# RWKV chunk inverse without GpSimd, and modulation blocks spread over all units, in a two-layer hybrid diffusion step

## What is computed

```python
m = silu(cond) @ w_mod + b_mod            # per layer, split in 6 vectors of 1024
kk = k * k_k;  kk = kk * rsqrt(sum(kk * kk) + 1e-12)
for d in (forward, backward):
    decay = exp(-exp(-softplus(-(w0[d] + tanh(h @ w1[d]) @ w2[d])) - 0.5))
    a = sigmoid(a0[d] + (h @ a1[d]) @ a2[d])
    k_d = k * (1 + (a - 1) * k_a)
    # scan over tokens, per head, S is 64x64:
    S = S * decay + (S @ -kk) (kk * a)^T + v k_d^T;   y = S @ r
```

## Time and profile before

| | |
|---|---|
| median of 3 runs | 2732.68 us (2728.0 to 2733.49) |
| the profiled execution | 2720.77 us, span of its instructions 2719.0 us, granted TensorE clock 0.975 |
| RWKV phases | about 300 to 635 us (layer 0) and 1465 to 1785 us (layer 1) |
| TensorE, VectorE, ScalarE, GpSimd busy | 92%, 53%, 39%, 11% |
| chain that ended last | TensorE 81%, VectorE 11%, issue 3%, ScalarE 3% |

### The profile page before, as it was taken

One profiled execution on the slowest core, in us unless ns is written; L12 is line 12 of the kernel. 1 busy time (PEld: TensorE's weight loads), 2 busy tenths in 40 slices (PEclk: granted clock), 3 DMA queues, 4 the chain that ended last, 5 costly groups with the idle time before them and its releaser, 6 DMA issues.

```text
span 2719.0 us, 67961 instructions
## 1 busy us (share of the span) xinstructions
PE 2492.1 (92%) x30324; PEld 2193.1 (81%) x30324; DVE 1449.9 (53%) x2522; ACT 1068.6 (39%) x1926; POOL 306.5 (11%) x307
## 2 busy tenths in 40 slices
PE   6998789988999999989987888888999999999996
PEld 3996577776798998969965767767999999999995
DVE  2337556666533333362375657665565555555565
ACT  3226433334421212242254334344444444444452
POOL 0002123330000000010011333301100000000011
PEclk8999899999999999989998999998999999999998
DMA  7223123200122222212200330002765666666572
GB/s 274 78 78 127 38 91 127 103 28 6 70 78 78 73 76 78 78 66 78 72 16 2 127 127 4 4 5 82 268 211 179 214 210 209 182 211 212 180 260 82
DMA packets 82700, 304.57 MB, mean 112 GB/s; under 512 B 9376, under 2 KB 9504, under 8 KB 82272
## 3 DMA queue, kind: packets, MB, share of 16 engines
q1 hardware_dynamic: 71072, 257.93, 28.8%
q0 software_dynamic: 11328, 42.21, 4.2%
HBM read 273.11 MB, written 27.00 MB: 110 GB/s over the span
## 4 chain that ended last, share of the span: by engine, by line
PE 81%; DVE 11%; issue 3%; ACT 3%; DMA 1%; POOL 1%; SPq 0%; DVEq 0%; ACTq 0%; POOLq 0%
PE ps L451 19%; PE ps L452 19%; PE ps L453 19%; PE ps L1181 6%; PE ps L464 2%; PE ps L915 2%; PE ps L810 1%; PE ps L958 1%; PE ps L1113 1%; PE ps L974 1%; DMA ring<-in_blocks 1%; PE ps L818 1%; DVE arena L2451 1%; DVE arena L2450 1%; PE ps L463 1%
## 5 line engine op out<-in xcount | busy, mean ns | idle before, releaser
L2258 DVE TENSOR_TENSOR ring_lo<-ring,w_ffn 128x1024 fp32r<-128x1024 f32 x264 | 322.4, 1225 | 214.4 <-ACT w_ffn L1700 208.7
L451 PE MATMUL ps<-hg_hi,w_ffn 128*128 128x256 f32 x1408 | 401.6, 285 | 0.9 <-DVE hg_lo L2891 0.9
L452 PE MATMUL ps<-hg_lo,w_ffn 128*128 128x256 f32 x1408 | 397.2, 282 | 0.0
L453 PE MATMUL ps<-hg_hi,ring_lo 128*128 128x256 f32 x1408 | 396.7, 282 | 0.0
L1700 ACT ACTIVATE w_ffn<-ring 128x1024 fp32r<-128x1024 f32 x264 | 278.2, 1057 | 197.8 <-PE ps L453 197.5
L451 PEld LDWEIGHTS ps<-hg_hi,w_ffn 128*128 128x128 f32 x1408 | 266.5, 189 | 2.6 <-DVE hg_lo L2891 1.1
L452 PEld LDWEIGHTS ps<-hg_lo,w_ffn 128*128 128x128 f32 x1408 | 265.6, 189 | 1.2
L453 PEld LDWEIGHTS ps<-hg_hi,ring_lo 128*128 128x128 f32 x1408 | 266.2, 189 | 0.0
L1181 PEld LDWEIGHTS ps<-arena 64*64 64x64 f32 x7680 | 168.8, 139 | 72.6 <-issue 63.1
L453 PE MATMUL ps<-hT_ffn_hi,ring_lo 128*128 128x320 f32 x704 | 215.5, 306 | 0.0
L451 PE MATMUL ps<-hT_hi,w_proj 128*128 128x320 f32 x672 | 205.7, 306 | 7.0 <-DVE hT_lo L2264 6.9
(11 more groups left out here) (379 smaller groups left out, 5205.0 us busy)
## 6 DMA issues: line engine op xcount, KB each, us to landing
ring<-in_blocks SPq DMA_DIRECT2D x484, 512.0 KB, 3.7
h_rows<-arena POOLq DMA_DIRECT2D x16, 512.0 KB, 10.2
arena<-h_rows POOLq DMA_DIRECT2D x7, 1024.0 KB, 11.1
y_rows<-arena POOLq DMA_DIRECT2D x7, 1024.0 KB, 6.6
x<-in_x_all SPq DMA_DIRECT2D x1, 2560.0 KB, 13.4
h_plain<-arena POOLq DMA_DIRECT2D x1, 2560.0 KB, 16.0
out_y_all<-x POOLq DMA_DIRECT2D x5, 512.0 KB, 3.6
w<-in_low POOLq DMA_DIRECT2D x2, 768.0 KB, 6.4
```

The costliest lines, as they stand in the source:

```text
L451: nc.tensor.matmul(dst, w_hi, m_hi, start=start, stop=False)
L452: nc.tensor.matmul(dst, w_hi, m_lo, start=False, stop=False)
L453: return nc.tensor.matmul(dst, w_lo, m_hi, start=False, stop=stop)
L2258: V.tensor_tensor(ring_lo[:, n % RING, :], ring[:, n % RING, :], high[:, n % high.shape[1], :], ALU.subtract).then_inc(*E.sig("w_lo"))
```

## The change

`plus_eye` is gone from GpSimd. ScalarE now copies N^T and N of both halves, and X of half 0; VectorE makes I + N^T of both halves, after ScalarE's copy, and copies X of half 1. VectorE's scan step now stands ahead of its work on the inverse in each slot. The copy to `qf` moves from VectorE to ScalarE. The scaled tanh of `prep` (L2560) moves to ScalarE, which writes it into `k_dec`; VectorE multiplies it by k in slot 5 instead of 6, and ScalarE's exponentials of slot 5, which overwrite `k_dec`, wait for that product. GpSimd keeps x0, lw and kds. In layer 0 an even unit has two groups of modulation and an odd one one; in layer 1 each unit has one. The blocks stand in slots 4 to 9, the rows in 7 and 10, the turns in 8 and 11. Each unit ends with a wait for its last modulation.

```diff
@@ slots and groups
+        def mod_groups(g):
+            if g is None:
+                return []
+            if g < UNITS:
+                at = MOD_FIRST + 3 * (g // 2) + 2 * (g % 2)
+                return [at, at + 1] if g % 2 == 0 else [at]
+            return [MOD_MID + g - UNITS]
+
+        def mod_slots(g):
+            return [((4, 4, 5, 6), 7, 8), ((6, 7, 8, 9), 10, 11)] if len(mod_groups(g)) == 2 else [((4, 6, 8, 9), 10, 11)]
@@ TensorE, rwkv_second
-                    if m0 is not None:
-                        if s == 4:
-                            if n is not None:
-                                pe.wait_ge(sem["ta_ev"], n + 1)
-                                pe.wait_ge(sem["vt_ev"], n // 2 + 1)
-                        if 4 <= s <= 7:
-                            for q in range(2):
-                                mod_block(2 * (s % 2) + q, 6 if s < 6 else 7)
-                        if s in (7, 8):
-                            mod_turn(m0 + s - 7, s - 1)
+                    if a is not None and s == 4 and n is not None:
+                        pe.wait_ge(sem["ta_ev"], n + 1)
+                        pe.wait_ge(sem["vt_ev"], n // 2 + 1)
+                    for k, (m, (blocks_at, row_at, turn_at)) in enumerate(zip(mod_groups(a), mod_slots(a))):
+                        for q in range(4):
+                            if blocks_at[q] == s:
+                                mod_block(q, 6 + k)
+                        if turn_at == s:
+                            mod_turn(m, 6 + k)
@@ ScalarE, decay_rest
-                A(kdt[:, :], pair640(src), ACT.Tanh, bias=..., scale=0.5).then_inc(*E.sig("ta_ev"))
+                A(kdt[:, :], pair640(src), ACT.Tanh, bias=..., scale=0.5).then_inc(*E.sig("act_step"))
+                act.wait_ge(*E.own_last())
+                if n >= 1:
+                    act.wait_ge(sem["tk_tr"], 3 * n)
+                A(k_dec[:, :], kdt[:, :], ACT.Identity, bias=hpar[:, 36 + c:37 + c], scale=hpar[:, 32 + c:33 + c]).then_inc(*E.sig("ta_ev"))
@@ ScalarE, exps, s == 5
                     act.wait_ge(sem["dec_cum"], 2 * n + 2)
+                    act.wait_ge(sem["kd_ev"], n + 1)
@@ ScalarE, rwkv_first, ahead of the copies of wu
+                    if d == 0:
+                        A(qf[:, 1, :], st_in[:, c, d, :], ACT.Copy).then_inc(*E.sig("qf_ev"))
+                    else:
+                        act.wait_ge(sem["dec_ph"], b + 1)
+                        A(qf[:, 1, :], st_in[:, c, d, :], ACT.Copy, scale=phs[:, b % 3, NCH:NCH + 1]).then_inc(*E.sig("qf_ev"))
@@ ScalarE, rwkv_second
-                    if a is not None and level <= 5 and half == 0:
-                        t, tx = half_tiles(0), x_tiles(0)
+                    if a is not None and level <= 5:
+                        t, tx = half_tiles(half), x_tiles(half)
                         act.wait_ge(sem["lv_mm"], LV_UNIT * a + s)
-                        A(by_head(nt_m[:, whole(t), :, :]), in_banks(0, 1, len(t)), ACT.Copy).then_inc(*E.sig("nt0_ev"))
+                        A(by_head(nt_m[:, whole(t), :, :]), in_banks(half, 1, len(t)), ACT.Copy).then_inc(*E.sig("nt_ev"))
                         if level <= 4:
+                            done = "n1_ev" if half else "lv0_ev" if level == 1 else "act_step"
+                            A(by_head(n_m[:, whole(t), :, :]), in_banks(half, 0, len(t)), ACT.Copy).then_inc(*E.sig(done))
-                        if level >= 2:
+                        if level >= 2 and half == 0:
                             A(by_head(xt[:, whole(tx), :, :]), in_banks(0, 2, len(tx)), ACT.Copy).then_inc(*E.sig("lv0_ev"))
@@ VectorE, rwkv_first: the copy to qf is gone; rwkv_second, behind the scan step
-                        V.tensor_copy(by_head(nt_m[:, whole(t), :, :]), in_banks(1, 1, len(t))).then_inc(*E.sig("nt1_ev"))
-                            V.tensor_copy(by_head(n_m[:, whole(t), :, :]), in_banks(1, 0, len(t))).then_inc(...)
+                    if a is not None and level <= 4:
+                        t = whole(half_tiles(half))
+                        dve.wait_ge(sem["nt_ev"], NT_UNIT * a + s)
+                        V.tensor_tensor(s_m[(level + 1) % 2][:, t, :, :], nt_m[:, t, :, :], eye_all[:, t, :, :], ALU.add).then_inc(*E.sig("s_ev"))
+                    if a is not None and 2 <= level <= 5 and half == 1:
+                        ...
+                        V.tensor_copy(by_head(xt[:, whole(tx), :, :]), in_banks(1, 2, len(tx))).then_inc(*E.sig("lv1_ev"))
@@ VectorE, prep
-                    V.tensor_scalar(kdt[:, :], kdt[:, :], hpar[:, 32 + c:33 + c], hpar[:, 36 + c:37 + c], ALU.mult, ALU.add).then_inc(*E.sig("dve_step"))
-                if s == 6:
-                    dve.wait_ge(*E.own_last_of("dve_step"))
-                    V.tensor_tensor(kdt[:, :], kdt[:, :], kr, ALU.mult).then_inc(*E.sig("kd_ev"))
+                    V.tensor_tensor(kdt[:, :], k_dec[:, :], kr, ALU.mult).then_inc(*E.sig("kd_ev"))
@@ GpSimd, rwkv_phase
-                        for s in range(1, 5):
-                            plus_eye(a, (s + 1) // 2, (s + 1) % 2)
-                    if a is not None:
-                        for s in range(5, 9):
-                            plus_eye(a, (s + 1) // 2, (s + 1) % 2)
```

## The result

The change makes the kernel slower: 2747.74 us (2743.95 to 2757.23) against 2728.26 (2722.34 to 2733.49), a ratio of 1.0078 with the interval 1.0063 to 1.0093. The forecast was 2725.3, its range ended at 2743. The profiled execution took 2743.95 us, span 2742.1.

The account below looks back on a forecast made before the run. The prediction took TensorE, busy 92% of the span, to bound the kernel. Its terms, -12.8 - 0.2 + 1.4 + 4.2 = -7.4 us, taken from 2732.7, gave 2725.3 us, range 2706 to 2743.

Parts of the forecast that it names:

- The second rival of the prediction: ScalarE's wait for the kd product does not bite, slot 8 stays at t = 14.9: 2709 us, chance 0.16.
- the placement: Modulation spread over the units, some blocks free in waits, 1.65 us more per one-group unit; -11.5 us in all.
- the inverse's later s8: I + N^T on VectorE, copies on ScalarE: slot 8 comes later in units without modulation before; +16 us in all.
- qf to ScalarE: Copy leaves VectorE, so L2487 follows L2474 at once: 0.85 us gained in each of 14 units.
- The walk to s8: Chain of handovers from prefix sums to slot 8: starts at t = 17.05 or 16.95 instead of 14.9, 2.1 us later.
- The price of a block: A modulation block costs TensorE 0.52 us, half of a pair's time; in slot 8, 0.38 of it is covered.
- Code: TensorE stops for its own code where short products stay dense behind slot 8: +4.2 us, between 0 and 16.
- the third rival: Code takes the gain: fewer waits turn into TensorE stops, one more of 0.9 us in 9 units; 2733 us, chance 0.14.
- Units of 38.0 and 39.0: Unit lengths in us with one and two modulation groups; units 1 to 6: -12.8 in layer 0, -0.2 in layer 1.
- First and last units: First unit of a layer unchanged; last unit's new modulation group partly fills TensorE's code stops, +0.7 us in each layer.
- The clock: TensorE's granted clock falling to its lower level: the prediction's sum had no term for it.
- The first rival: The new chain costs more: slot 8 another 1.5 us later in 14 units, 21 us; 2746 us, chance 0.22.

Follow-up runs that it names:

- e3: The kernel before with only the copy to qf moved from VectorE to ScalarE; ratio to before 0.9975.
- e10: The kernel before with the qf copy on ScalarE and the modulation spread as in the change, old inverse kept; ratio to before 0.9985.
- e7: The change with lw made by VectorE and GpSimd's three kds operations cut to 64 of 640 columns, leaving out most of the bonus term; ratio to before 1.0040.
- e15: The change with one modulation block of each one-group unit in slot 7 instead of slot 8; ratio to before 1.0000.
- e18: The change with modulation blocks in pairs, the second pair of one-group units in slot 7; ratio to before 1.0104.
- e11: The change with the modulation group of each layer's last unit moved into an earlier unit; ratio to before 1.0046.
- e6: The change with its modulation blocks put in pairs, two to a slot; ratio to before 1.0124.

## Why the prediction was wrong, step by step

The profile gives the whole account for RWKV: forecast -7.4, measured +17.75 (584.5 to 602.25), a miss of 25.2. The span adds 5.4 outside of RWKV, which is within the scatter named above.

The ratios say which part the miss stands in. The second rival of the prediction (s8 as before) had -23.4 us in all, so the forecast was -11.9 for qf, -11.5 for the placement and +16 for the inverse's later s8. Measured were -6.9 (e3), +2.7 (e10 over e3) and +25.4 (the change over e10). Of the 28.7 us of miss 14 lie in the placement, 9 in the inverse, 5 in qf.

**qf to ScalarE (-0.85 a unit): right in the mechanism.** L2499 now starts 0.74 us behind L2491, where the earlier trace rows had 1.59 from L2474 to L2487:

```profile
1687.94 0.82 DVE L2491 TENSOR_TENSOR arena<-ps,small 128x640 f32<-128x640 f32 x1
...
1688.68 0.55 DVE L2499 TENSOR_TENSOR arena<-ps,con 128x384 f32<-128x384 f32 x1
```

Alone it won 6.9 us by the ratio and 12.9 in the RWKV phases of the profile (584.5 to 571.6), for 12 of the sum.

**The walk to s8 (+2.1): right.** Forecast t = 17.05 and 16.95, measured 16.8 and 17.0 in the units with one group, by the links that were named, the lock of the ports among them (2.05 and 2.70 for 0.81 and 1.55), though VectorE's product was held and not its sum of s5. The rule of the Trainium skill (SBUF — State Buffer, "SBUF: two separate sides") that was weighed against the change held, and e7 gave it a price, some 10 us net of the 0.8 us a unit that lw then takes of VectorE. What was left out is what a bare wait brings besides its length, the clock and the block that stands behind it and not in it: e15 won 21 us without moving s8. In layer 1, 6.5 of its 12.85 are products at the higher clock (3.7 and 2.8).

**The price of a block (0.52, s8's for 0.14): wrong, the largest term.** The earlier trace rows hold eight rows for two blocks, and I halved their 1.06. A block makes its products for two of the four 32-row strips of the output, `ps[32 * t:32 * t + 32]` with t = 2q and 2q + 1, modulo 4, and the next block those for the other two. So two neighbours can run side by side, and one alone takes as long as both. The kernel before had single ones in its first 40 us, a row that I didn't read:

```profile
29.23 1.05 PE L810 MATMUL ps<-ring,cond 128*32 128x512 f32 x4 [0.22 <-DMA ring<-in_blocks]
```

At full clock 32 blocks cost 33.7 for 17.0, +16.7 a layer. The Trainium skill has this: in TensorEngine Tiling (Array Packing), "Tiling Modes", an array of 128x32 tiles is four that can run in parallel. The trace agrees, 1.05 for one block and 1.06 for two.

**Code (+4.2): wrong in sign in the change, right as a rival under pairs.** Layer 1's stops without a releaser fell by 9.2 instead of growing. They fell in e10 too (9.9), so it is the single blocks that did it; that a block gives code time to arrive, 1 us for four rows of products, is argued. That gave back about half of the block term of 16.7. With pairs the blocks gave back 14.9 and the stops took 22.3. "A gain by fewer waits turns into stops" was the third rival's text; it came true for a saving of block time, in e18. The "mostly hidden" that the Trainium skill has for such a crossing (Runtime: NRT & Kernel Launch, "Instruction fetch mechanics") does not fit this kernel: the stops without a releaser are 18.5 us of layer 1's phase before and 32.0 in e18.

**Units of 38.0 and 39.0: right for three units of twelve, and there by luck.** With a block at 1.05 the two that the sum took as exposed make 39.1 of the 38.0. Against that, the 35.1 that it starts from is a unit at 1.2 GHz behind s8: three groups of 40 rows take 1.34, 1.29 and 1.25 us there, and 0.81, 0.81 and 0.76 in the three units of 38.0. I took that for the unit's own length. With two groups 40.9, 43.9 and 41.95, each 1.9 to 4.9 too long: s8's turn and up to five single blocks were priced at the halved rate or as hidden. Units 1 to 6 of layer 0 came to +3.6 for -12.8, of layer 1 to +7.2 for -0.2, before the 4.2 for code.

**First and last units (0, and +0.7 each): wrong.** The first unit of layer 0, which has its two groups as before but in the new slots, took +3.2, that of layer 1, with one group less, -0.3. The last took +2.5 and +3.2. A group of four blocks (4.2) and a turn (1.0) stands there beside nothing; the stops of the earlier trace rows took up only half of that. With the old inverse they cost the same (21.8 and 23.6 in e10), without a group they are back at 19.5 (e11).

**The clock: no term.** By its column TensorE had the lower level for some 25 and 18 us of the two phases, in before for 30 and 11 (twice the share missing times the length). The change lost nothing to it against before. But it lost to what it could have been: the same placement with the old inverse has 0.99 in both (e10).

So the miss of 25.2 is 16.4 in layer 0's units, 7.4 in layer 1's, 4.3 in the last ones and 1.2 in what is left (+2.8 in the first units, -1.7 for qf ahead of the last), less the 4.2 for code that stood apart. The first rival's time (2746) was near by luck, not by its reason: it was to decide only if s8 came later than 17.95.

## What to carry to other kernels

Price a piece of work by a row in which it stands as it will stand, alone or beside its neighbour; half of a pair is no price where the pair runs in parallel strips of TensorE's array. When an edit moves a wait, put independent work that TensorE has to do anyway straight into the new wait: the same block one slot earlier was worth 0.78% here with the new inverse and nothing with the old. Where TensorE stops and the view names no releaser, look whether a transfer of the instruction queue began shortly before. And time the small parts alone: of three edits only the copy moved off VectorE paid.

## What the runs showed of the hardware that I had not expected

- A modulation block of four rows lasts 1.05 us alone, two next to each other 1.06 together.
- TensorE fell to 1.2 GHz for 6.8 us in a slot where it had stood 1.26 us and then 0.6 us of a stop of 1.54; the unit behind kept 2.4 GHz through one stop of 1.61. With pairs of blocks (e6) its mean in layer 1's RWKV phase was 0.91, with one block in the wait (e15) 1.00, for the same products.
- TensorE waits for its code. The stops for which the profile gives no releaser end 2.2 to 2.9 us after a 16 KB transfer of the instruction queue began (all 65 of 0.6 us or more in the phases of seven kernels), and 64 of these stand multiples of 256 of its instructions apart. All such stops come to 9.3 us in one layer's phase in the change, 18.5 before and 32.0 with pairs (e18), single ones up to 3.3 us.
- A VectorE product of 640 columns took 2.05 us beside GpSimd's subtraction, which took 2.70 for the 1.55 that it takes alone: both lose, in turn. The subtraction's 1.15 more is near the 1.36 of the two VectorE operations that ran at full speed beside it (0.55 and 0.81).
